# Six hosted matmul groups packed into 16 rounds each: a hybrid attention and short-convolution block on one core

## The chip, the cores and the metric

The program runs on one core of a Trainium2 chip. The metric is the device time of one execution in microseconds (us). The engines are TensorE (PE, matmuls, with its weight loads listed apart as PEld), VectorE (DVE), ScalarE (ACT), GpSimd (POOL) and SyncE (SP, which here only issues DMAs). Each works through its own list in order and waits on semaphores for the others.

## The reference

One layer of a streaming encoder. 16 meta tokens are put ahead of 256 input rows of width 2048, the rows are RMS-normalised, and one large projection makes everything that follows:

```
h = rmsnorm(x, norm_g)
proj = einsum('bld,dn->bln', h, w_in)          # w_in: 2048 x (10 * 2048 + 16)
(q, k, v, f_logit, z_att, u, gate_b, gate_c, z_conv, m_att, m_conv) = split(proj)
y_att  = (forgetting_attention(q, k, v, log_sigmoid(f_logit + b_f)) * silu(z_att)) @ w_att_o
y_conv = (gate_b * short_conv(gate_c * u, conv_w) * silu(z_conv)) @ w_conv_o
merged = sigmoid(m_att) * y_att + sigmoid(m_conv) * y_conv
return x + merged @ w_out                      # then a last rmsnorm
```

All data are float32. The kernel gets float32 accuracy out of a rounded format by splitting each operand into a high and a low part and summing three products: high x high, high x low, low x high.

## The kernel before

The part that the change touches is the first half of the program, the short-convolution stage. Its work comes in **units**. A unit is 512 KB of `w_in` (four blocks of 128 rows, 256 columns). For each unit SP loads it into one of 4 raw buffers (`load_conv`), ACT copies it to the rounded high part `w_hi` (L651), DVE subtracts to get the low part `w_lo` (L1025), and PE multiplies (24 matmuls of 258 columns on L1445 to L1447 in a pair's first 8 units, 16 on L1459 and L1460 in its last 8). 16 units make one **pair** of 128-channel blocks: u, gate_c, gate_b and z_conv with 4 units each. There are 8 pairs, 128 units. Around a pair's units lie small side operations on ACT and DVE that take the projections out of PSUM and do the convolution: on DVE `cu` (L1128), two adds (L1146, L1148), two operations on `joined` (L1132, L1135), one more (L1139), the gate (L1152, L1154) and the low part of the result (L1158).

Three other projections, m_conv, m_att and z_att, do not have a stage of their own. They are **hosted**: cut into six **groups** of 1024 columns, computed by a seven-product scheme for 2 x 2 blocks (Strassen's, in Winograd's form), and inserted between the units of the convolution. A group has 16 **steps**, one after a unit. The first 8 steps (its A half, at the rounds in `A_AFTER`) have 9 matmuls of 512 columns each, the last 8 (the B half, `B_AFTER`) have 12. Here a **round** is one unit with the step behind it, if it has one; the number of a round counts from the group's first unit. A step's weights (a quad of four 512-column blocks) are loaded into one of 3 buffers, DVE forms sums of blocks in place (one sum, L1037, in an A step; three that follow one another, L1039, L1041, L1043, in a B step), ACT rounds (L659 and L663, or L667 and L670), and DVE splits (L1050 and L1055, or L1059 and L1062).

The products of a group add up in four PSUM banks (P1, P2, P5, P7). Between its halves ACT copies P1 and P5 out (L742, L745) and DVE adds P2 (L1166, semaphore `c11_made`) before PE may begin the B half. At the group's end ACT copies P1 (L751, semaphore `u2_kept`), DVE makes four blocks (L1173, L1176, L1180, L1184; `c21_made` comes with the third), and PE may begin the next group. These places are set by `group_at(n, offset)`: ACT and DVE do them in round `offset` of the group, after that round's own rounding and splitting.

What sets the order is a set of tables and the loops over n in each engine's block: `GROUP_UNITS`, `A_AFTER`, `B_AFTER`, and `sums_after`, which says in which round of DVE the parts of a step's sum are made. In DVE's loop a round is: sums, the unit's split, the step's splits, side operations of the pair, and then the copies out of a group. ACT and DVE run ahead of PE, but at most five slots: `w_hi` and `w_lo` have `CONV_RING` = 5 slots in this stage, a unit takes one and a step two, and ACT waits on `w_used` for the slot five before.

Before the change a group takes `GROUP_UNITS` = 18 units. 16 have a step behind them; the units of round 8 and round 17 are **free**, with no step. After the six groups (units 16 to 123) four units are left.

Of the kernel before, what the change touches and what calls it, by code (L numbers as in the profile page):

```python
# [65 lines left out]
N_CONV, N_F, N_ATT, N_OUT = 4 * PER, 2, 3 * PER, 2 * KT  # L66
# [1 line left out]


GROUPS, GROUP_COLS = 6, 1024  # L70
GROUP_UNITS = (CONV_UNITS - N_CONV) // GROUPS
STEPS = KT // 2
A_AFTER = (0, 1, 2, 3, 4, 5, 6, 7)
B_AFTER = (9, 10, 11, 12, 13, 14, 15, 16)
STEP_AFTER = A_AFTER + B_AFTER
GROUP_SLOTS = GROUP_UNITS + 2 * len(STEP_AFTER)
CONV_RING, QUADS = 5, 3
# [88 lines left out]
def group_at(n, offset):  # L166

    g, r = divmod(n - N_CONV - offset, GROUP_UNITS)
    return g if r == 0 and 0 <= g < GROUPS else None
# [33 lines left out]
def hybrid_block(nc, x, meta_tokens, norm_gain, w_in, b_f, conv_w, w_att_o, w_conv_o, w_out,  # L203
# [131 lines left out]
    with ExitStack() as ctx:  # L335
# [258 lines left out]
        def _(act):  # L594
# [88 lines left out]
            for n in range(LEAD + 1, CONV_UNITS + LEAD + 1):  # L683
# [50 lines left out]
                if n == 14:  # L734
                    round_sum(S4, sum_t0[:, 1, :, :])

                g = group_at(n, A_AFTER[-1] + 2)
                if g is not None:
                    act.wait_ge(w_used, RING + step_slot(g, STEPS - 1) + 2)
                    if g > 0:  # L740
# [2 lines left out]
                    if g > 0:  # L743
                        act.wait_ge(c22_made, g)
                    nc.scalar.copy(p5[:], ps[:, P5_BANK, :]).then_inc(p5_kept, 1)  # L745
                g = group_at(n, B_AFTER[-1] + 2)
                if g is not None:
                    act.wait_ge(w_used, RING + step_slot(g, 2 * STEPS - 1) + 2)
                    if g > 0:
# [150 lines left out]
        def _(dve):  # L900
# [210 lines left out]
            for n in range(LEAD + 1, CONV_UNITS + LEAD + 1):  # L1111
# [48 lines left out]
                                            ).then_inc(o_split, 1)  # L1160
                make_sums(n)

                g = group_at(n, A_AFTER[-1] + 2)
                if g is not None:
                    dve.wait_ge(p1_kept, g + 1)
                    nc.vector.tensor_tensor(stage[0][:], stage[0][:], ps[:, P2_BANK, :], ALU.add  # L1166
                                            ).then_inc(c11_made, 1)
                g = group_at(n, B_AFTER[-1] + 2)
                if g is not None:
                    dve.wait_ge(u2_kept, g + 1)  # L1170
                    if g > 0:
# [205 lines left out]
        def _(pe):  # L1377
# [144 lines left out]
            def strassen_step(g, step):  # L1522

                c, s = step_slot(g, step), step % STEPS
                first, last_one = s == 0, s == STEPS - 1
                left, right = slice(0, HALF), slice(HALF, UNIT)
                one = lambda cols: (w_hi[:, hi_slot(c), cols], w_lo[:, lo_slot(c), cols])
                two = lambda cols: (w_hi[:, hi_slot(c + 1), cols], w_lo[:, lo_slot(c + 1), cols])
                p1, p2, p5_, p7 = (ps[:, bank, :] for bank in (P1_BANK, P2_BANK, P5_BANK, P7_BANK))
                if step < STEPS:  # L1530
                    if first:
                        pe.wait_ge(s_split, 1)
                        if g > 0:
                            pe.wait_ge(c21_made, g)
                    pe.wait_ge(w_split, RAW + c + 1)
                    product(p1, *h_piece(0, 2 * s), *one(left), start=first, stop=last_one)
                    product(p2, *h_piece(0, 2 * s + 1), *one(right), start=first, stop=last_one).then_inc(w_used, 1)
                    pe.wait_ge(w_split, RAW + c + 2)
                    product(p5_, *sum_piece(S1, s), *two(left), start=first, stop=last_one).then_inc(w_used, 1)
                else:  # L1540
                    if first:
                        pe.wait_ge(s_split, 4)
                        pe.wait_ge(c11_made, g + 1)
                        pe.wait_ge(p5_kept, g + 1)
                    pe.wait_ge(w_split, RAW + c + 1)
                    product(p1, *sum_piece(S2, s), *one(left), start=False, stop=last_one, resumed=True)
                    product(p7, *sum_piece(S3, s), *one(right), start=first, stop=last_one).then_inc(w_used, 1)
                    pe.wait_ge(w_split, RAW + c + 2)
                    product(p2, *h_piece(1, 2 * s + 1), *two(left), start=first, stop=last_one)
                    product(p5_, *sum_piece(S4, s), *two(right), start=False, stop=last_one, resumed=True  # L1550
                            ).then_inc(w_used, 1)
# [182 lines left out]
```

## Time and profile before

| | us |
|---|---|
| median of 3 runs (lowest, highest) | 1215.01 (1214.58, 1215.49) |
| the profiled execution's own time | 1215.36 |
| its span, first to last instruction | 1213.4 |
| PE busy | 1196.0 |
| DVE busy | 956.8 |
| ACT busy | 649.9 |

The span is cut by the profiler's first and last instruction; the 2 us between it and the execution's own time lie around it. A matmul that follows another is started before that one has ended, so starts, not durations, show how fast PE goes. A row of the timeline gives the start in us from the span's start, the duration, the engine and line, what is written and read, and in brackets the idle time just before it and what ended it.

### The profile page before, as it was taken

The numbers are of one execution on the slowest core, as the hardware profiler recorded it, in microseconds if no ns is written. First come the engines' busy times: TensorE is split into PE (matmuls) and PEld (weight loads), VectorE is DVE, ScalarE is ACT, GpSimd is POOL, SyncE is SP. The second block draws the span as 40 slices with busy tenths as digits, with TensorE's granted clock in tenths as the row PEclk, the third lists the DMA queues.
The fourth block names the chain that finished last, engine by engine and source line by source line (L and its number), as shares of the span: only waits on it lengthen the run. The fifth ranks groups of instructions, "written<-read, shape, count | busy, mean of one in ns | idle before, by whom it ended". The sixth has DMA issues, their size and how long they took to land.

```text
span 1213.4 us, 18388 instructions
## 1 busy us (share of the span) xinstructions
PE 1196.0 (99%) x7225; PEld 1068.2 (88%) x7225; DVE 956.8 (79%) x1116; ACT 649.9 (54%) x865; POOL 35.7 (3%) x50
## 2 busy tenths in 40 slices
PE   7999999999999999999999999999999999999997
PEld 7998898898888988889888899999999999888885
DVE  6889988988989989989966546877787778755544
ACT  6666555556656566656555444444544554543532
POOL 1000000000000000000000010111011101000000
PEclk9999999999999999999999999999999999999999
DMA  6798898897898888888677866555655565765663
GB/s 215 217 299 279 268 295 268 272 302 258 272 291 286 269 293 282 271 302 265 196 240 262 269 187 182 149 171 168 208 153 172 152 204 164 224 207 178 214 227 114
DMA packets 181393, 280.40 MB, mean 231 GB/s; under 512 B 9312, under 2 KB 128176, under 8 KB 180912
## 3 DMA queue, kind: packets, MB, share of 16 engines
q1 hardware_dynamic: 172000, 263.78, 68.2%
q10 hardware_dynamic: 9312, 15.49, 4.1%
q8 instruction: 57, 0.93, 0.3%
q14 instruction: 24, 0.20, 0.1%
HBM read 270.83 MB, written 8.41 MB: 230 GB/s over the span
## 4 chain that ended last, share of the span: by engine, by line
PE 89%; DVE 8%; issue 1%; ACT 1%; DMA 0%; POOLq 0%; POOL 0%; SPq 0%; DVEq 0%; ACTq 0%
PE ps L1445 22%; PE ps L1447 22%; PE ps L1446 22%; PE ps L1459 13%; PE ps L1460 7%; DVE w_lo L1025 2%; DVE w_lo L1062 1%; DVE w_lo L1059 1%; DVE quads L1041 1%; DVE quads L1043 1%; DVE quads L1039 1%; DMA x_nat<-in_x 0%; PE ps L1468 0%; PE ps L1439 0%; PE ps L1613 0%
## 5 line engine op out<-in xcount | busy, mean ns | idle before, releaser
L909 DVE TENSOR_TENSOR w_lo<-w_raw,w_hi 128x1024 fp32r<-128x1024 f32 x197 | 239.7, 1235 | 99.1 <-ACT w_hi L603 98.4
L1445 PE MATMUL ps<-h,w_hi 128*128 128x258 f32 (+1 forms) x1024 | 294.2, 287 | 1.6 <-DVE w_lo L1025 0.9
L1446 PE MATMUL ps<-h,w_hi 128*128 128x258 f32 (+1 forms) x1024 | 291.7, 285 | 0.0
L1447 PE MATMUL ps<-h,w_lo 128*128 128x258 f32 (+1 forms) x1024 | 291.5, 285 | 0.0
L1459 PE MATMUL ps<-h,w_hi 128*128 128x512 f32 x768 | 273.3, 398 | 0.3 <-DVE w_lo L1025 0.3
L603 ACT CAST w_hi<-w_raw 128x1024 fp32r<-128x1024 f32 x198 | 203.3, 1049 | 112.6 <-PE ps L1447 65.6
L1460 PE MATMUL ps<-h,w_lo 128*128 128x256 f32 x768 | 215.4, 280 | 0.0
L1445 PEld LDWEIGHTS ps<-h,w_hi 128*128 128x128 f32 x1024 | 193.3, 189 | 5.4 <-issue 1.9
L1446 PEld LDWEIGHTS ps<-h,w_hi 128*128 128x128 f32 x1024 | 193.5, 189 | 1.9
L1447 PEld LDWEIGHTS ps<-h,w_lo 128*128 128x128 f32 x1024 | 193.4, 189 | 0.0
L1459 PEld LDWEIGHTS ps<-h,w_hi 128*128 128x128 f32 x768 | 144.2, 188 | 35.5 <-DVE w_lo L1025 1.0
L1025 DVE TENSOR_TENSOR w_lo<-w_raw,w_hi 128x1024 fp32r<-128x1024 f32 x122 | 148.7, 1220 | 16.1 <-ACT w_hi L651 16.0
L1460 PEld LDWEIGHTS ps<-h,w_lo 128*128 128x128 f32 x768 | 145.0, 189 | 1.8
L651 ACT CAST w_hi<-w_raw 128x1024 fp32r<-128x1024 f32 x122 | 126.9, 1050 | 25.6 <-PE ps L1447 25.6
L667 ACT CAST w_hi<-quads 128x1024 fp32r<-128x1024 f32 x48 | 50.6, 1053 | 109.3 <-DVE quads L1041 102.2
L1445 PE MATMUL ps<-w_hi,o 128*128 128x512 f32 x256 | 100.2, 391 | 0.0
L1447 PE MATMUL ps<-w_hi,o 128*128 128x512 f32 x256 | 99.7, 389 | 0.0
L1446 PE MATMUL ps<-w_lo,o 128*128 128x512 f32 x256 | 99.6, 389 | 0.0
L1445 PE MATMUL ps<-w_hi,s_hi 128*128 128x512 f32 x192 | 75.6, 394 | 0.0
L1447 PE MATMUL ps<-w_hi,s_lo 128*128 128x512 f32 x192 | 75.3, 392 | 0.0
L1446 PE MATMUL ps<-w_lo,s_hi 128*128 128x512 f32 x192 | 74.8, 390 | 0.0
L663 ACT CAST w_hi<-quads 128x512 fp32r<-128x512 f32 x48 | 29.8, 622 | 64.0 <-PE ps L1447 32.2
(197 smaller groups left out, 1827.5 us busy)
## 6 DMA issues: line engine op xcount, KB each, us to landing
w_raw<-in_w_in SPq DMA_DIRECT2D x226, 512.0 KB, 4.8
quads<-in_w_in SPq DMA_DIRECT2D x144, 512.0 KB, 4.4
w_raw<-in_w_conv_o SPq DMA_DIRECT2D x32, 512.0 KB, 5.6
w_raw<-in_w_att_o SPq DMA_DIRECT2D x32, 512.0 KB, 4.8
w_raw<-in_w_out SPq DMA_DIRECT2D x32, 512.0 KB, 4.7
quads<-in_w_in SPq DMA_DIRECT2D x48, 256.0 KB, 4.7
gates_dram<-stage ACTq DMA_DIRECT2D x24, 256.0 KB, 4.8
gate_nat<-gates_dram ACTq DMA_DIRECT2D x8, 512.0 KB, 4.2
```

What stands on the lines that cost most here:

```text
L603: nc.scalar.copy(w_hi[:, hi_slot(c), :], w_raw[:, c % RAW, :]).then_inc(w_rounded, 1)
L651: nc.scalar.copy(w_hi[:, hi_slot(c), :], w_raw[:, n % RAW, :]).then_inc(w_rounded, 1)
L663: nc.scalar.copy(w_hi[:, hi_slot(c + 1), 0:HALF], quads[:, q, 0, HALF:]).then_inc(w_rounded, 1)
L667: nc.scalar.copy(w_hi[:, hi_slot(c), :], quads[:, q, 0, :]).then_inc(w_rounded, 1)
L909: nc.vector.tensor_tensor(w_lo[:, lo_slot(c), :], w_raw[:, c % RAW, :], w_hi[:, hi_slot(c), :].bitcast(F32), ALU.subtract).then_inc(w_spli ...
L1025: nc.vector.tensor_tensor(w_lo[:, lo_slot(c), :], w_raw[:, n % RAW, :], w_hi[:, hi_slot(c), :].bitcast(F32), ALU.subtract).then_inc(w_spli ...
L1039: nc.vector.tensor_tensor(b12, b22, b12, ALU.subtract).then_inc(t_made, 1)
L1445: nc.tensor.matmul(dst, a_hi, b_hi, start=start, stop=False, skip_group_check=resumed)
L1446: nc.tensor.matmul(dst, a_hi, b_lo, start=False, stop=False, skip_group_check=resumed)
L1447: return nc.tensor.matmul(dst, a_lo, b_hi, start=False, stop=stop, skip_group_check=resumed)
L1459: nc.tensor.matmul(dst, a_hi, b, start=start, stop=False)
L1460: return nc.tensor.matmul(dst[:, HI, :], a_lo, b[:, HI, :], start=False, stop=stop)
```

## The change

A group takes 16 units, each with a step, so there are no free units: the B half is in rounds 8 to 15, and the next group follows at once. The groups then lie on the pairs, units 16 to 111, and the last pair's 16 units have no group. The copies out of PSUM move from two rounds after a half's last step to one round after. The wait for `c21_made` at a group's first step moves from its first product to its second; the first product now waits for `u2_kept`. With `B_AFTER` beginning right behind `A_AFTER`, the function `sums_after` puts all three parts of the first B step's sum in round 8 itself.

```diff
@@ -68,10 +68,10 @@
 
 
 GROUPS, GROUP_COLS = 6, 1024
-GROUP_UNITS = (CONV_UNITS - N_CONV) // GROUPS
+GROUP_UNITS = 16
 STEPS = KT // 2
 A_AFTER = (0, 1, 2, 3, 4, 5, 6, 7)
-B_AFTER = (9, 10, 11, 12, 13, 14, 15, 16)
+B_AFTER = (8, 9, 10, 11, 12, 13, 14, 15)
 STEP_AFTER = A_AFTER + B_AFTER
 GROUP_SLOTS = GROUP_UNITS + 2 * len(STEP_AFTER)
 CONV_RING, QUADS = 5, 3
@@ -734,7 +734,7 @@
                 if n == 14:
                     round_sum(S4, sum_t0[:, 1, :, :])
 
-                g = group_at(n, A_AFTER[-1] + 2)
+                g = group_at(n, A_AFTER[-1] + 1)
                 if g is not None:
                     act.wait_ge(w_used, RING + step_slot(g, STEPS - 1) + 2)
                     if g > 0:
@@ -743,7 +743,7 @@
                     if g > 0:
                         act.wait_ge(c22_made, g)
                     nc.scalar.copy(p5[:], ps[:, P5_BANK, :]).then_inc(p5_kept, 1)
-                g = group_at(n, B_AFTER[-1] + 2)
+                g = group_at(n, B_AFTER[-1] + 1)
                 if g is not None:
                     act.wait_ge(w_used, RING + step_slot(g, 2 * STEPS - 1) + 2)
                     if g > 0:
@@ -1160,12 +1160,12 @@
                                             ).then_inc(o_split, 1)
                 make_sums(n)
 
-                g = group_at(n, A_AFTER[-1] + 2)
+                g = group_at(n, A_AFTER[-1] + 1)
                 if g is not None:
                     dve.wait_ge(p1_kept, g + 1)
                     nc.vector.tensor_tensor(stage[0][:], stage[0][:], ps[:, P2_BANK, :], ALU.add
                                             ).then_inc(c11_made, 1)
-                g = group_at(n, B_AFTER[-1] + 2)
+                g = group_at(n, B_AFTER[-1] + 1)
                 if g is not None:
                     dve.wait_ge(u2_kept, g + 1)
                     if g > 0:
@@ -1531,9 +1531,11 @@
                     if first:
                         pe.wait_ge(s_split, 1)
                         if g > 0:
-                            pe.wait_ge(c21_made, g)
+                            pe.wait_ge(u2_kept, g)
                     pe.wait_ge(w_split, RAW + c + 1)
                     product(p1, *h_piece(0, 2 * s), *one(left), start=first, stop=last_one)
+                    if first and g > 0:
+                        pe.wait_ge(c21_made, g)
                     product(p2, *h_piece(0, 2 * s + 1), *one(right), start=first, stop=last_one).then_inc(w_used, 1)
                     pe.wait_ge(w_split, RAW + c + 2)
                     product(p5_, *sum_piece(S1, s), *two(left), start=first, stop=last_one).then_inc(w_used, 1)
```

How this moves instructions is shown at three places. `quads` is the buffer of a step's weights, `w_hi` and `w_lo` the two parts, `ps` PSUM.

DVE in group 0 where the B half begins. Before, two units (two L1025) lie between the start of the first sum and the step's splits:

```order
L1039 TENSOR_TENSOR quads<-quads 128x512 [waits quad_landed2]
L1041 TENSOR_TENSOR quads<-quads 128x512 [waits t_made]
L1025 TENSOR_TENSOR w_lo<-w_raw,w_hi 128x1024 [waits w_rounded]
L1043 TENSOR_TENSOR quads<-quads 128x512 [waits t_made]
L1025 TENSOR_TENSOR w_lo<-w_raw,w_hi 128x1024 [waits w_rounded]
L1059 TENSOR_TENSOR w_lo<-quads,w_hi 128x1024 [waits w_rounded]
L1062 TENSOR_TENSOR w_lo<-quads,w_hi 128x1024 [waits w_rounded]
L1128 TENSOR_TENSOR cu<-ps,u_sb 128x516 [waits free_a,w_used]
L1166 TENSOR_TENSOR stage_90<-stage_90,ps 128x512 [waits p1_kept]
```

and after the change:

```order
L1039 TENSOR_TENSOR quads<-quads 128x512 [waits quad_landed2]
L1041 TENSOR_TENSOR quads<-quads 128x512 [waits t_made]
L1043 TENSOR_TENSOR quads<-quads 128x512 [waits t_made]
L1025 TENSOR_TENSOR w_lo<-w_raw,w_hi 128x1024 [waits w_rounded]
L1059 TENSOR_TENSOR w_lo<-quads,w_hi 128x1024 [waits w_rounded]
L1062 TENSOR_TENSOR w_lo<-quads,w_hi 128x1024 [waits w_rounded]
L1166 TENSOR_TENSOR stage_90<-stage_90,ps 128x512 [waits p1_kept]
L1039 TENSOR_TENSOR quads<-quads 128x512 [waits quad_landed0]
```

One L1025 is gone, the three parts of the sum stand together ahead of the unit, and the copy out (L1166) comes before the side operation L1128, which has moved into the next round.

DVE at the end of group 0. Before:

```order
L1025 TENSOR_TENSOR w_lo<-w_raw,w_hi 128x1024 [waits w_rounded]
L1139 TENSOR_TENSOR joined<-ps,joined 128x512 [waits low_kept]
L1037 TENSOR_TENSOR quads<-quads 128x512 [waits z_joined,quad_landed1]
L1025 TENSOR_TENSOR w_lo<-w_raw,w_hi 128x1024 [waits w_rounded]
L1050 TENSOR_TENSOR w_lo<-quads,w_hi 128x1024 [waits w_rounded]
L1055 TENSOR_TENSOR w_lo<-quads,w_hi 128x512 [waits w_rounded]
L1173 TENSOR_TENSOR stage_91<-stage_92,ps 128x512 [waits u2_kept]
L1176 TENSOR_TENSOR stage_92<-stage_92,ps 128x512 [waits c12_made]
L1180 TENSOR_TENSOR stage_90<-stage_92,ps 128x512 [waits gate_stored0,v_made]
L1184 TENSOR_TENSOR stage_92<-stage_92,p_93 128x512 [waits p5_kept,c21_made]
L1037 TENSOR_TENSOR quads<-quads 128x512 [waits quad_landed2]
L1025 TENSOR_TENSOR w_lo<-w_raw,w_hi 128x1024 [waits w_rounded]
```

After the change:

```order
L1062 TENSOR_TENSOR w_lo<-quads,w_hi 128x1024 [waits w_rounded]
L1037 TENSOR_TENSOR quads<-quads 128x512 [waits quad_landed1]
L1025 TENSOR_TENSOR w_lo<-w_raw,w_hi 128x1024 [waits w_rounded]
L1050 TENSOR_TENSOR w_lo<-quads,w_hi 128x1024 [waits w_rounded]
L1055 TENSOR_TENSOR w_lo<-quads,w_hi 128x512 [waits w_rounded]
L1173 TENSOR_TENSOR stage_91<-stage_92,ps 128x512 [waits u2_kept]
L1176 TENSOR_TENSOR stage_92<-stage_92,ps 128x512 [waits c12_made]
L1180 TENSOR_TENSOR stage_90<-stage_92,ps 128x512 [waits gate_stored0,v_made]
L1184 TENSOR_TENSOR stage_92<-stage_92,p_93 128x512 [waits p5_kept,c21_made]
L1037 TENSOR_TENSOR quads<-quads 128x512 [waits quad_landed2]
L1025 TENSOR_TENSOR w_lo<-w_raw,w_hi 128x1024 [waits w_rounded]
```

The free unit (the first L1025 before) and a round with a step no longer stand ahead of L1173: the four blocks now come in the first round of the next group, and L1139 one round behind them.

PE at the first step of group 1. Before:

```order
L1447 MATMUL ps<-h,w_lo 128x258
L1445 MATMUL ps<-w_hi,h 128x512 [waits w_split,c21_made,s_split]
L1446 MATMUL ps<-w_lo,h 128x512
L1447 MATMUL ps<-w_hi,h 128x512
L1445 MATMUL ps<-w_hi,h 128x512
L1446 MATMUL ps<-w_lo,h 128x512
```

After the change:

```order
L1447 MATMUL ps<-h,w_lo 128x258
L1445 MATMUL ps<-w_hi,h 128x512 [waits w_split,u2_kept,s_split]
L1446 MATMUL ps<-w_lo,h 128x512
L1447 MATMUL ps<-w_hi,h 128x512
L1445 MATMUL ps<-w_hi,h 128x512 [waits c21_made]
L1446 MATMUL ps<-w_lo,h 128x512
```

The first product waits for ACT's copy alone, and the second for DVE's third block.

## Rows read from the trace of the kernel before

**Rows 1.** The page, section 1: busy time, share of the span and instructions.

```profile
PE 1196.0 (99%) x7225; PEld 1068.2 (88%) x7225; DVE 956.8 (79%) x1116; ACT 649.9 (54%) x865; POOL 35.7 (3%) x50
```

**Rows 2.** Waits of PE, whole span: waiting line, releaser, total us, times, longest.

```profile
PE ps L1468 <- DMA x_nat<-in_x: 7.4, 1, 7.4
PE ps L1445 <- DVE w_lo L1025: 0.9, 1, 0.9
...
PE ps L1459 <- DVE w_lo L1025: 0.3, 1, 0.3
```

**Rows 3.** Windows: length, busy PE, PEld, DVE, ACT, POOL (instructions), clock, DMA share, GB/s.

```profile
107.60:152.46 44.86, 44.86 (x235) 37.97 (x234) 44.16 (x52) 27.32 (x33) 0.00 (x0) 1.00 0.84 270
...
65.35:603.79 538.44, 537.17 (x3171) 473.97 (x3169) 497.86 (x578) 322.18 (x391) 0.00 (x0) 1.00 0.85 275
```

**Rows 4.** Timeline of PE, group 0: first matmuls of units and steps.

```profile
99.88 0.28 PE L1445 MATMUL ps<-h,w_hi 128*128 128x258 f32 x1
...
102.74 0.39 PE L1445 MATMUL ps<-w_hi,h 128*128 128x512 f32 x1
...
104.81 0.39 PE L1459 MATMUL ps<-h,w_hi 128*128 128x512 f32 x1
...
107.62 0.40 PE L1459 MATMUL ps<-h,w_hi 128*128 128x512 f32 x1
...
110.45 0.40 PE L1445 MATMUL ps<-w_hi,s_hi 128*128 128x512 f32 x1
...
113.19 0.39 PE L1459 MATMUL ps<-h,w_hi 128*128 128x512 f32 x1
...
118.79 0.39 PE L1459 MATMUL ps<-h,w_hi 128*128 128x512 f32 x1
...
135.62 0.50 PE L1459 MATMUL ps<-h,w_hi 128*128 128x512 f32 x1
```

**Rows 5.** Timeline of DVE, group 0, end of A half and B half.

```profile
99.32 0.68 DVE L1039 TENSOR_TENSOR quads<-quads 128x512 f32<-128x512 f32 x1
...
107.21 0.68 DVE L1166 TENSOR_TENSOR stage<-stage,ps 128x512 f32<-128x512 f32 x1
107.81 0.68 DVE L1039 TENSOR_TENSOR quads<-quads 128x512 f32<-128x512 f32 x1
...
109.86 1.22 DVE L1025 TENSOR_TENSOR w_lo<-w_raw,w_hi 128x1024 fp32r<-128x1024 f32 x1
...
113.27 0.68 DVE L1039 TENSOR_TENSOR quads<-quads 128x512 f32<-128x512 f32 x1
...
118.73 0.68 DVE L1146 TENSOR_TENSOR conv<-conv,conv 128x512 f32<-128x512 f32 x1
...
120.06 0.68 DVE L1039 TENSOR_TENSOR quads<-quads 128x512 f32<-128x512 f32 x1
...
130.97 0.68 DVE L1132 TENSOR_TENSOR joined<-ps,joined 128x512 f32<-128x512 f32 x1
...
132.30 0.68 DVE L1039 TENSOR_TENSOR quads<-quads 128x512 f32<-128x512 f32 x1
...
134.35 1.22 DVE L1025 TENSOR_TENSOR w_lo<-w_raw,w_hi 128x1024 fp32r<-128x1024 f32 x1
```

**Rows 6.** Timeline of ACT, group 0, where the B half begins.

```profile
103.00 1.05 ACT L667 CAST w_hi<-quads 128x1024 fp32r<-128x1024 f32 x1 [1.55 <-PE ps L1447]
...
105.33 0.58 ACT L742 COPY stage<-ps 128x512 f32<-128x512 f32 x1
```

**Rows 7.** Timeline of DVE, copies out at the end of group 0.

```profile
154.13 0.68 DVE L1173 TENSOR_TENSOR stage<-stage,ps 128x512 f32<-128x512 f32 x1
...
156.89 0.69 DVE L1037 TENSOR_TENSOR quads<-quads 128x512 f32<-128x512 f32 x1
...
160.37 0.68 DVE L1152 TENSOR_TENSOR gate<-joined,gate 128x512 f32<-128x512 f32 x1
```

**Rows 8.** Timeline of PE, group 2, the longest wait of the stage.

```profile
328.60 0.36 PE L1445 MATMUL ps<-h,w_hi 128*128 128x258 f32 x1 [0.85 <-DVE w_lo L1025]
```

## The prediction

> **What bounds the kernel now.** I read the page first: PE is busy for 1196.0 of 1213.4 us and DVE for 956.8 [rows 1]. Then the waits of PE: of the little idle time 7.4 us is the first load, and only 1.2 us lies in the stage that hosts the groups, both times behind DVE's split of a unit, L1025 [rows 2]. Then the windows: over the hosted stretch, 65.35 to 603.79, PE is busy for all but 1.27 us, while in a B half (107.60 to 152.46) DVE is busy for 44.16 of 44.86 us, 98% [rows 3]. So PE sets the end everywhere, with DVE right behind it in the B halves. The change removes no matmul and adds none. It can give back at most the 1.3 us of waits, and the question is how much lead over PE it takes from DVE.
>
> **The two paces.** From the starts in PE's timeline [rows 4]: a unit of 24 matmuls takes 102.74 - 99.88 = 2.86 us, one of 16 takes 107.62 - 104.81 = 2.81, an A step 104.81 - 102.74 = 2.07 (nine matmuls, 0.23 each), a B step 113.19 - 110.45 = 2.74, and a whole B round 118.79 - 113.19 = 5.60. From DVE's starts [rows 5]: a B round takes 113.27 - 107.81 = 5.46, namely 2.05 for the three sums (to 109.86) and 3.41 for three splits, 1.14 each. A 512-column operation by itself takes 0.60 (107.21 to 107.81); the pair's side operations that come two by two take 1.33 (118.73 to 120.06, and 130.97 to 132.30). An A round takes DVE 160.37 - 156.89 = 3.48 [rows 7] against PE's 4.93. So in a B round DVE gains 0.14 us, and every side operation in a B half costs lead. DVE starts a B half with all the lead that the five slots allow: ACT itself waited 1.55 us for PE there [rows 6].
>
> A rule speaks of just this number. The Trainium skill says in "VectorE: DVE Perf Modes", section "The DRAIN you can't avoid", that the next operation does not start until the pipeline is empty. The splits here last 1.22 us and start 1.14 apart [rows 5], so the trace does not bear it out. By the rule a B round would cost DVE about 0.26 us more (three splits by 0.08), some 12 us over 48 rounds. I go by the starts.
>
> **Check of the method on before.** Unit 10 of group 0 starts at 113.19 [rows 4], and its split is done at 109.86 + 1.22, seen by PE about 0.05 later: a lead of 2.06 us. To unit 14 DVE needs four rounds and two double side operations, 4 x 5.46 + 2 x 1.33 = 24.5, PE 22.4: a loss of 2.10. The lead should be just gone at unit 14. It is: the split of unit 14 ends at 134.35 + 1.22 = 135.57 [rows 5], and PE starts it at 135.62, its first matmul 0.50 instead of 0.39 long [rows 4].
>
> **Part 1: no free unit before the B half.** Up to 99.32, where DVE begins the first B step's sum, nothing changes in group 0. Then, after the change: three sums to 101.37, the unit's split to 102.51, the step's first split to 103.65. The second waits for ACT's rounding, which waits for the slot of unit 7: done at 102.74, seen 0.26 later as in [rows 6], rounding 1.05, so DVE goes on at 104.09 and is through at 105.23. Next is the copy out L1166. It waits for ACT's copy of P1, which needs the last A step (done at 104.81): 104.81 + 0.26 + 0.58 + 0.04 = 105.69. DVE idles 0.46, and begins the sums of round 9 at 106.29. The bank is ready at 106.4, and PE begins the B half at 104.81 + 2.81 = 107.62, so this wait costs PE nothing. Unit 9 is split at 106.29 + 2.05 + 1.22 + 0.05 = 109.61, and PE wants it at 107.62 + 2.74 = 110.36. The lead is 0.75 us, where it was 2.06 at the matching place.
>
> From unit 9 to unit 14 DVE needs 5 x 5.46 + 0.60 + 1.33 + 1.33 = 30.56 us (L1128 now lies behind unit 9) and PE 28.00, a loss of 2.56. PE must wait 2.56 - 0.75 = 1.8 us per B half: by rounds 0.75 at unit 12, behind the two adds, and 1.05 at unit 14, behind the two operations on `joined`. All six groups have this alignment, since group and pair both take 16 units.
>
> **Part 2: the copies out in the next group's first round.** PE ends the B half at T, then does unit 0 (2.86) and step 0 (2.07), and wants unit 1 at T + 4.93. DVE has done unit 0's splits and stands at L1173 until ACT has copied P1: T + 0.26 + 0.58 + 0.04. Its four operations take 156.89 - 154.13 = 2.76 [rows 7]. The third, which releases the second product of step 0, ends at about T + 3.05. PE reaches step 0 at T + 2.86 and that product 0.69 later, so the moved wait hides it; with the old wait it would cost 0.2 us at each of five places. What is queued behind is the sum (0.60) and the split of unit 1, seen at T + 0.88 + 2.76 + 0.60 + 1.27 = T + 5.5. PE waits 0.6 us, in five groups. After this the A half lets DVE win back about 1.45 us a round, so the next B half begins from full slots again.
>
> **Part 3: behind the last group** no step follows unit 0 of the last pair, so PE wants unit 113 at T + 2.86, while its split (no sum ahead) is there at T + 4.9: a wait of 2.05, once. The other 15 plain units cost DVE 1.14 each plus side operations against PE's 2.8, and nothing waits. The loads move with their rounds. Each quad still waits for the splits of the step three before; SP has no new order within a round, and the DMA share of the stage is 0.85 [rows 3]. I cost them at nothing; two rounds of DVE, 10.9 us, lie between that split and the next use of the buffer, which hides them.
>
> **Sum.** 5 x (1.8 + 0.6) + 1.8 + 2.05 = 15.8 us of waits by starts. Before has 1.27 idle, and each wait also hides what is left of the matmul before it (0.39 - 0.23 = 0.16), with smaller ones not visible: I take 2.0, within 1.3 and 2.7. Net +13.8. The profiled execution took 1215.36, its span 1213.4 and 2 us around it that do not change: 1229.1. It lies 0.35 above the median of the runs, so I forecast 1228.8.
>
> What no row shows is DVE at L1166 waiting for ACT. Its idle could be from 0 (ACT's copy is ready, as it was before) to 1.05 (one more rounding ahead of it), 0.46 from the rows; that is -0.5 to +0.6 on each of six leads, -3 to +4 us. The wait at L1173 has bounds of 0 idle (the unit's split and 0.6 us of wait gone: -3 - 0.9) and the same 1.05 more (+6). Both ends together are unlikely.
>
> **Rivals.**
> Not slower: the lead at unit 9 stays as deep as the slots allow. If DVE had 2.56 us or more there, all six B halves would run as group 0 does now, groups 1 and 2 would lose their waits of today, and the time would be 1215.0 - 1.3 = 1213.7, or within 0.2% with the waits of part 2. For it speaks that group 0, with this alignment, has almost none today. Against it speaks where the lead comes from: the free unit gives PE 2.81 us of work and DVE 1.14, and that goes. It decides at 2.56 against my 0.75.
>
> Half the price: only one of the two waits of a B half appears and ACT's copies come early, 7 us: 1222.
>
> The banks become the bound: if the copies out end a microsecond later than worked out, PE waits at 11 half-group starts for the bank itself and DVE starts each half with 1 us less lead. That is 11 us more: 1240. The margins against it are 1.2 us at the B half and 0.5 at the second product.
>
> The clock: the longest wait of the stage now, 0.85 us [rows 8], left the granted clock at 1.00, 2.4 GHz, over the whole stretch [rows 3]. If some 18 waits of 0.6 to 2 us each brought one round at the lower level, twice as long, that would be 18 x 5.6 = 100 us, 1329. The Trainium skill, in "TensorE: Matmul & The Clock Gate", section "A second HAM failure mode: psum-queue depth-cycling", tells of a kernel whose frequent short idles between groups of matmuls made the clock swing. By that rule this would be the outcome; the trace does not show it so far.
>
> **How the numbers follow.** The forecast has 0.74, not slower 0.06 (half of it within 0.2%), half the price 0.09, the banks 0.09, the clock 0.02. About 0.2%, 2.4 us, is what a measurement can tell. Faster 0.03, same 0.04, slower 0.93. The forecast's own range is 1225 to 1233; half the price and part of the banks' case widen it to 1222 to 1235.
>
> **What would show it.** In the profile after: waits of PE for L1025 of some 15 us in total, three in each group (units 12, 14, and 1 of the next), and one of about 2 us in the last pair; DVE without idle in the B halves but for about 0.5 us at L1166; a clock of 1.00; no wait on L1166 or L1180. Wrong would be: no waits at units 12 and 14, PE waits released by stage copies, or a growth outside the hosted stretch.

## The result, and the profile after

The changed kernel takes 1230.56 us, median of 4 runs (1228.49 to 1230.96), against 1215.10 of the kernel before in the same rounds (1214.58 to 1215.49): 1.0124 times as long, 95% interval 1.0112 to 1.0136. It is slower by 15.5 us, where 13.8 were forecast. The profiled execution took 1230.9 us, its span 1228.9.

Line 1 of the page after, to be held against [rows 1]:

```profile
PE 1200.9 (98%) x7225; PEld 1068.9 (87%) x7225; DVE 958.5 (78%) x1116; ACT 648.8 (53%) x865; POOL 35.7 (3%) x50
```

The counts of instructions have not changed. On the chain that ended last DVE's share rose from 8% to 18%, PE's fell from 89% to 78%.

```profile
PE 78%; DVE 18%; issue 2%; ACT 1%; DMA 0%; POOLq 0%; POOL 0%; SPq 0%; DVEq 0%; ACTq 0%
```

The waits of PE in the profile after (line, releaser, total, times, longest). Against 1.2 us in the hosted stretch before [rows 2] there are 12.1, in 18 places, all behind DVE's split of a unit:

```profile
PE ps L1459 <- DVE w_lo L1025: 8.4, 12, 0.8
PE ps L1468 <- DMA x_nat<-in_x: 7.3, 1, 7.3
PE ps L1445 <- DVE w_lo L1025: 3.7, 6, 1.8
```

The stage they are in, from the windows of the profile after (stretch, its length, busy PE, PEld, DVE, ACT, POOL, granted clock, DMA share, GB/s). The first row is the six groups. The second is the first eight units of the last pair, and the third a piece of that, whose granted clock is 0.57 on average: for 3.41 of its 3.94 us the clock was at the lower of the two levels (1.2 instead of 2.4 GHz). The last row is all that follows the convolution:

```profile
65.29:584.39 519.10, 508.83 (x2930) 442.89 (x2929) 481.29 (x559) 304.80 (x369) 0.00 (x0) 1.00 0.84 275
584.39:610.89 26.50, 24.67 (x193) 24.45 (x192) 15.83 (x17) 12.50 (x15) 0.00 (x0) 0.94 0.70 218
589.26:593.20 3.94, 3.94 (x20) 3.94 (x21) 3.54 (x4) 2.53 (x3) 0.00 (x0) 0.57 0.69 178
633.50:1228.90 595.40, 587.39 (x3586) 528.05 (x3584) 398.26 (x453) 282.55 (x405) 31.62 (x34) 1.00 0.61 190
```

From the first hosted unit to the end of the convolution the kernel before takes 617.91 - 65.35 = 552.56 us, the changed one 633.50 - 65.29 = 568.21: 15.65 us more. The rest takes 595.5 in both (1213.4 - 617.9 and 1228.9 - 633.5). So the whole difference lies in the hosted stretch and the last pair.

Inside a group, PE's starts in group 0 of the profile after (start, duration, instruction; in brackets the idle time before it and what ended it):

```profile
110.34 0.39 PE L1459 MATMUL ps<-h,w_hi 128*128 128x512 f32 x1
...
121.53 0.39 PE L1459 MATMUL ps<-h,w_hi 128*128 128x512 f32 x1
...
127.91 0.47 PE L1459 MATMUL ps<-h,w_hi 128*128 128x512 f32 x1 [0.62 <-DVE w_lo L1025]
...
133.58 0.39 PE L1459 MATMUL ps<-h,w_hi 128*128 128x512 f32 x1
...
140.06 0.50 PE L1459 MATMUL ps<-h,w_hi 128*128 128x512 f32 x1 [0.72 <-DVE w_lo L1025]
...
151.30 0.28 PE L1445 MATMUL ps<-h,w_hi 128*128 128x258 f32 x1
...
156.76 0.39 PE L1445 MATMUL ps<-h,w_hi 128*128 128x258 f32 x1 [0.37 <-DVE w_lo L1025]
```

These are units 9, 11, 12, 13, 14, and 0 and 1 of the next group. A B round is 5.60 us of PE's work [rows 4]. The round from 121.53 to 127.91 takes 6.38, the one from 133.58 to 140.06 takes 6.48: PE loses 0.78 and 0.88 us. From 151.30 to 156.76 it needs 5.46 for work of 4.93: 0.53 lost. The brackets show less (0.62, 0.72, 0.37), since the matmul ahead of a wait is drawn out to its full 0.39 us, of which 0.16 lie beside the next one when nothing waits. The sum is 2.2 us. The groups' starts lie 86.01 us apart once and then 86.57 to 86.64, against 8 x 4.93 + 8 x 5.60 = 84.2 of work: 2.4 us a group.

DVE's timeline of the same place, to be held against [rows 5]:

```profile
99.27 0.68 DVE L1039 TENSOR_TENSOR quads<-quads 128x512 f32<-128x512 f32 x1
...
102.45 1.22 DVE L1059 TENSOR_TENSOR w_lo<-quads,w_hi 128x1024 fp32r<-128x1024 f32 x1
104.02 1.23 DVE L1062 TENSOR_TENSOR w_lo<-quads,w_hi 128x1024 fp32r<-128x1024 f32 x1 [0.35 <-ACT w_hi L670]
105.57 0.69 DVE L1166 TENSOR_TENSOR stage<-stage,ps 128x512 f32<-128x512 f32 x1 [0.32 <-ACT stage L742]
106.17 0.68 DVE L1039 TENSOR_TENSOR quads<-quads 128x512 f32<-128x512 f32 x1
...
108.22 1.22 DVE L1025 TENSOR_TENSOR w_lo<-w_raw,w_hi 128x1024 fp32r<-128x1024 f32 x1
```

The two idles of 0.35 and 0.32 are the waits for ACT that the working had put at 0.44 and 0.46. The split of unit 9 ends at 109.44 and PE wants it at 110.34: a lead of 0.85 us, once 0.05 is taken off for the signal. Before it was 2.06 us at the matching place.

### The profile page after: what moved, and what is told of

The parts are those of the page before. It is cut to its first block, busy times and chain, and to the rows that moved or that the text cites. A ratio compares the mean times of both kernels' runs of the same rounds, so it can differ in the third digit from the quotient of the medians.

```text
span 1228.9 us, 18388 instructions
## 1 busy us (share of the span) xinstructions
PE 1200.9 (98%) x7225; PEld 1068.9 (87%) x7225; DVE 958.5 (78%) x1116; ACT 648.8 (53%) x865; POOL 35.7 (3%) x50
## 4 chain that ended last, share of the span: by engine, by line
PE 78%; DVE 18%; issue 2%; ACT 1%; DMA 0%; POOLq 0%; POOL 0%; SPq 0%; DVEq 0%; ACTq 0%
PE ps L1445 20%; PE ps L1447 20%; PE ps L1446 20%; PE ps L1459 10%; PE ps L1460 5%; DVE w_lo L1025 4%; DVE w_lo L1062 3%; DVE w_lo L1059 2%; DVE quads L1041 2%; DVE quads L1043 2%; DVE quads L1039 2%; DMA x_nat<-in_x 0%; PE ps L1468 0%; DVE stage L1173 0%; DVE stage L1176 0%
## 5 line engine op out<-in xcount | busy, mean ns | idle before, releaser
L1445 PE MATMUL ps<-h,w_hi 128*128 128x258 f32 (+1 forms) x1024 | 295.3, 288 | 4.3 <-DVE w_lo L1025 3.7
L1445 PEld LDWEIGHTS ps<-h,w_hi 128*128 128x128 f32 x1024 | 194.0, 189 | 9.0 <-DVE w_lo L1025 6.0
L1025 DVE TENSOR_TENSOR w_lo<-w_raw,w_hi 128x1024 fp32r<-128x1024 f32 x122 | 148.4, 1220 | 14.9 <-ACT w_hi L651 14.6
L1445 PE MATMUL ps<-w_hi,o 128*128 128x512 f32 x256 | 100.2, 391 | 0.0
L1445 PE MATMUL ps<-w_hi,s_hi 128*128 128x512 f32 x192 | 75.8, 395 | 0.0
```

The lines of the kernel that those rows point to most:

```text
L1025: nc.vector.tensor_tensor(w_lo[:, lo_slot(c), :], w_raw[:, n % RAW, :], w_hi[:, hi_slot(c), :].bitcast(F32), ALU.subtract).then_inc(w_spli ...
L1445: nc.tensor.matmul(dst, a_hi, b_hi, start=start, stop=False, skip_group_check=resumed)
```

## The experiments

The kernels ran in three batches, each beside runs of the kernel before, with medians of 1214.66, 1214.84 and 1214.56 us. Ratios are to these, with 95% intervals.

**The changed kernel again.**

> The changed kernel again, unchanged, as the yardstick of this chip and to see the clock. Theory: the last pair's single wait of 1.8 us idle lets TensorE's clock fall for 3.41 us in most executions, and one without the fall is some 1.6 us faster (1228.5 to 1229 us at a mean clock of 0.998) than one with it (1230.2 to 1231 us at 0.995 to 0.996). If the spread of the earlier runs has another cause, time and mean clock will not go together.

Measured: 1228.83 us (1228.65 to 1230.25), ratio 1.0122 (1.0105 to 1.0139). Its waits are those of the first profile to 0.2 us. What differs most is the last pair. The windows of this run's profile, over the eight units and over the piece behind the 1.8 us wait:

```profile
584.02:609.00 24.98, 23.14 (x194) 22.93 (x192) 15.83 (x17) 12.49 (x15) 0.00 (x0) 1.00 0.74 230
588.89:592.80 3.91, 3.91 (x32) 3.91 (x33) 3.50 (x4) 2.52 (x3) 0.00 (x0) 1.00 0.69 185
```

Here 32 matmuls run in 3.91 us at the full clock, in the first profile 20 in 3.94 at the lower one, and the eight units take 24.98 instead of 26.50. So the fall costs 1.5 us, and it is no fixed part of the kernel. The expectation had it in most executions. Of these four, the profiled one did not have it, and three lie within 0.3 us of each other (1228.65 to 1228.91). Without the fall the changed kernel takes 1228.8 us. This run is what the others are compared with below.

The mean clock of a whole run, which the expectation wanted to go by, does not tell where the clock fell. The profile after has a second low piece ahead of the hosted stretch, and the profile before, in which nothing was changed, has one in the same place. Windows of the first and of the second:

```profile
16.35:19.76 3.41, 3.41 (x19) 3.41 (x18) 3.41 (x10) 2.30 (x6) 0.00 (x0) 0.50 0.07 11
```
```profile
16.30:19.71 3.41, 3.41 (x18) 3.41 (x18) 3.41 (x10) 2.31 (x6) 0.00 (x0) 0.50 0.06 9
```

The repetition has none there. So its span is shorter than that of the first profile (1226.7 against 1228.9) by more than the last pair's fall: 1.5 us are that fall, 0.4 lie in the last pair's other eight units (22.61 against 22.18 us, cause open), 0.7 ahead of the first hosted unit (65.29 against 64.56), and the six groups take 0.4 us more in the repetition (519.46 against 519.10).

**The last group's copies out one round later.** Only for the group that no group follows.

```diff
+def copies_at(n):
+
+    g = group_at(n, B_AFTER[-1] + 1)
+    if g == GROUPS - 1:
+        return None
+    return GROUPS - 1 if group_at(n, B_AFTER[-1] + 2) == GROUPS - 1 else g
...
-                g = group_at(n, B_AFTER[-1] + 1)
+                g = copies_at(n)
```

> The changed kernel, with the copies out of the last group alone made one round later on ACT and DVE, so that unit 113 is split before them. My theory: the wait of 2.0 us at unit 113 goes, unit 114 gets no new one (its split is seen at T + 4.85, wanted at T + 5.7), and with the wait goes the fall of the clock: 3.6 us less than the changed kernel, about 1227.0, and a mean clock of 0.998 in every run. If the clock fell for another reason (what lies behind the last group, or the sum of the small waits), 2.0 us less, about 1228.6, and still a fall. If the wait was the load's and not the split's place in the order, no difference.

Measured: 1226.95 us (1226.47 to 1227.54), ratio 1.0101 (1.0084 to 1.0118). The waits of PE in this profile (its lines are 8 further down):

```profile
PE ps L1467 <- DVE w_lo L1033: 8.4, 12, 0.8
PE ps L1453 <- DVE w_lo L1033: 1.9, 5, 0.4
```

Of six waits on the second line five are left, and the longest is 0.4 instead of 1.8. The eight units take 22.87 us, by their starts 585.03 and 607.90, instead of 24.98. So part 3 is right: L1173 to L1184 ahead of unit 113's split cost 2.0 us, once. The time is the expected 1227.0, but that is 1.9 us less than the repetition; the expected 3.6 counted from 1230.6 and had the clock's fall in it. As the repetition has no fall either, this run does not show that the wait brings it.

**The groups ten units later in the pairs.** Groups and units stay as after the change; only the side operations of a pair fall into other rounds.

```diff
+FIRST_HOST = N_CONV + 10
-    if n < N_CONV:
+    if n < FIRST_HOST:
...
-    return divmod(n - N_CONV, GROUP_UNITS) if N_CONV <= n else (-1, n)
+    return divmod(n - FIRST_HOST, GROUP_UNITS) if FIRST_HOST <= n else (-1, n)
```

> The changed kernel with all groups begun 10 units later (units 26 to 121), everything else equal: the same 16 rounds, but in a B half DVE now has the gate's two operations in round 9, L1158 in round 12 and L1128 in round 15, instead of L1128, two adds and two operations on joined in rounds 9, 11 and 13. My theory (pace and lead of DVE): lead 0.85 us at unit 9, then 1.33 + 0.60 of side operations less 0.14 a round before unit 13: 0.5 us of waits per B half instead of 1.7 to 1.8, so 7.5 us less than the changed kernel, about 1223. Rival (what matters is that steps follow without a free unit: banks, loads or the five slots): the waits stay whatever the side operations do, 1230.

Measured: 1224.11 us (1223.12 to 1225.77), ratio 1.0083 (1.0067 to 1.01). Its waits:

```profile
PE ps L1460 <- DVE w_lo L1026: 5.0, 6, 1.9
PE ps L1446 <- DVE w_lo L1026: 1.5, 6, 0.2
```

The kernel is 4.7 us faster than the repetition, where 7.5 were expected, and a group takes 85.70 us instead of 86.70. By PE's starts against a round's work (5.59 to 5.61 us in a B half, 4.91 to 4.93 in an A half), the six B halves lose 4.4 us in all where the repetition loses 11.3. That is 0.7 a group; the expectation had 0.5. But unit 1 of the next group now loses 0.75 instead of 0.54, and once 1.03: 4.0 in all instead of 2.7. So where the side operations fall decides some 60% of what the B halves lose and, with what is lost again at unit 1, about a third of the whole price. The rival, under which the waits stay whatever the side operations do, is out.

**The old wait back.** PE waits for `c21_made` at the first product again.

```diff
-                            pe.wait_ge(u2_kept, g)
+                            pe.wait_ge(c21_made, g)
...
-                    if first and g > 0:
-                        pe.wait_ge(c21_made, g)
```

> The changed kernel with the wait for c21_made back on the first product of a group's first step. My prediction counted 0.2 us at each of five places for this, about 1 us in all (1231.5). From the trace of the changed kernel I now think nothing is lost: PE would begin the step some 0.15 us later, but then waits 0.15 us less for unit 1, whose split DVE sets: 1230.5, the same group length of 86.6 us.

Measured: 1229.16 us (1228.13 to 1229.8), ratio 1.0122 (1.0105 to 1.0139), and groups 86.70 us apart, as in the repetition. The waits:

```profile
PE ps L1459 <- DVE w_lo L1025: 8.5, 12, 0.8
PE ps L1445 <- DVE w_lo L1025: 1.8, 1, 1.8
```

The five waits at unit 1 are gone and the time stays as it was: the later start of step 0 only uses up the time in which PE would have waited for unit 1. Moving the wait was worth nothing.

**The two adds left out.** The conv taps' two sums on DVE (L1146, L1148).

```diff
-                    nc.vector.tensor_tensor(conv[0][:], conv[0][:], conv[1][:], ALU.add).then_inc(conv_step, 1)
-                    dve.wait_ge(conv_step, steps + 1)
-                    nc.vector.tensor_tensor(conv[0][:], conv[0][:], conv[2][:, :, 0:SEQ], ALU.add
-                                            ).then_inc(conv_step, 1)
+                    dve.sem_inc(conv_step, 2)
```

> The changed kernel without the pair's two adds (L1146, L1148), on any engine; the sums over the three taps are left out of the output. After the adds on GpSimd made the kernel slower (1231.5), this tells the cause apart. My theory: a B-half wait is DVE's work less its lead, so 1.33 us less per group: no wait at unit 12, about 0.4 at unit 14, 8 us less than the changed kernel: 1221. If ACT's rounding or the banks set units 12 and 14, no change: 1229.

Measured: 1221.77 us (1220.28 to 1222.76), ratio 1.0055 (1.004 to 1.0071). Its waits, and PE at unit 14:

```profile
PE ps L1442 <- DVE w_lo L1025: 3.7, 6, 1.8
PE ps L1456 <- DVE w_lo L1025: 1.6, 6, 0.3
```
```profile
137.59 0.50 PE L1456 MATMUL ps<-h,w_hi 128*128 128x512 f32 x1 [0.27 <-DVE w_lo L1025]
```

The wait at unit 12 is gone and that at unit 14 down to 0.27 us, 0.42 by starts, as expected; a group takes 85.30 us, where it takes 86.63 in the first profile and 86.70 in the repetition: 1.33 to 1.40 less. Two such operations cost DVE 1.33 [rows 5], so they are passed on to PE in full. The six groups together are 8.2 us shorter than in the repetition. The median is lower by only 7.1: in the profiled run (1221.63) the clock fell behind the last pair's 1.8 us wait too, which costs 1.5.

**One operation twice, in the B half and in the A half.** A 512-column product repeated at L1135 (round 13, inside the B half) and, in another kernel, at L1154 (round 3, inside the A half).

```diff
+                    nc.vector.tensor_tensor(conv_gated[:], joined[:], conv[0][:], ALU.mult).then_inc(twice, 1)
+                    dve.wait_ge(twice, pair + 1)
```
```diff
+                    nc.vector.tensor_tensor(prod2[:], gate[:], conv_gated[:], ALU.mult).then_inc(twice, 1)
+                    dve.wait_ge(twice, pair + 1)
```

> The changed kernel with L1135 done twice (round 13, inside every B half). My theory: DVE has no lead left there, so the second time costs its full 0.72 us in each of six groups and nothing in the first and last pair: 4.3 us more, 1233.1. If the slots hid it: 1229.

> The changed kernel with L1154 done twice (round 3, inside every A half). The same length of work on the same engine, 0.72 us in five A halves. My theory: DVE gains 1.45 us of lead a round there and starts the B half from full slots all the same: no change, 1228.8. If the group's whole DVE work set its length, 3.6 us more: 1232.4.

Measured: in the B half 1233.36 us (1232.64 to 1233.97), ratio 1.015 (1.0134 to 1.0165); in the A half 1228.41 (1227.62 to 1229.65), ratio 1.0114 (1.0099 to 1.013). The waits of the first and of the second:

```profile
PE ps L1462 <- DVE w_lo L1026: 12.7, 12, 1.5
PE ps L1448 <- DVE w_lo L1026: 3.7, 6, 1.8
```
```profile
PE ps L1462 <- DVE w_lo L1026: 8.4, 12, 0.8
PE ps L1448 <- DVE w_lo L1026: 3.7, 6, 1.8
```

The same kind of work costs 4.5 us in one place and nothing in the other. A part of the 4.5 is the clock, which fell in the profiled run (1233.97; the two fastest are 1232.64 and 1232.78). By their starts (64.32 and 588.01) the six groups take 523.69 us instead of 519.46: 4.2 more, 0.70 for each. Unit 14's wait grew from 0.8 to 1.5. This is the plainest evidence for the account by leads: DVE's work counts in the B half, and not in round 3 of the A half, where DVE has time to spare. (Right behind the copies, in rounds 0 and 1, it counts too, as the waits at unit 1 show.)

**A free unit back, in the middle or at the end.** Groups of 17 units. In the first kernel the free unit stands before the B half, in the second between the groups.

```diff
-GROUP_UNITS = 16
+GROUP_UNITS = 17
-B_AFTER = (8, 9, 10, 11, 12, 13, 14, 15)
+B_AFTER = (9, 10, 11, 12, 13, 14, 15, 16)
...
-                g = group_at(n, A_AFTER[-1] + 1)
+                g = group_at(n, A_AFTER[-1] + 2)
```
```diff
-GROUP_UNITS = 16
+GROUP_UNITS = 17
...
-                g = group_at(n, B_AFTER[-1] + 1)
+                g = group_at(n, B_AFTER[-1] + 2)
```

> Half of the change: groups of 17 units with the free unit before the B half put back (B half in rounds 9 to 16, copies two rounds behind the A half, as before), and none between groups. My theory: the B-half waits fall from 1.8 us a group to what the kernel before has at such positions (3 us over all six, since the groups drift by one unit against the pairs), while the waits behind the copies at a group's end stay: 0.6 in five groups and 2.0 once. 1212.7 without waits + 3 + 3 + 2 = 1220.7. If the B-half waits came from the missing unit between the groups instead, it would stay near 1227.

> The other half: groups of 17 units with the free unit between groups put back, and the B half right behind the A half as in the changed kernel. My theory: no waits behind the copies at a group's end and none of 2 us at the last (5 us less than the changed kernel), B-half waits of 1.4 to 2.1 us a group, 10.8 in all: 1212.7 + 10.8 = 1223.5. The rival that the end copies set the pace: 1216 to 1218.

Measured: 1222.74 us (1222.15 to 1223.34), ratio 1.0068 (1.0053 to 1.0084), and 1224.1 us (1224.0 to 1224.26), ratio 1.0078 (1.0063 to 1.0094). The waits of the first and of the second:

```profile
PE ps L1445 <- DVE w_lo L1025: 5.3, 7, 1.8
PE ps L1459 <- DVE w_lo L1025: 1.5, 4, 0.8
```
```profile
PE ps L1459 <- DVE w_lo L1025: 6.3, 9, 1.1
PE ps L1445 <- DVE w_lo L1025: 0.9, 1, 0.9
```

Each free unit takes away the waits of its own kind. These rows sort by PE's line and not by place: on L1445 lie the waits at unit 1 as well as those of a B half that falls on a pair's first eight units. Such are these two, at unit 100 in the first kernel and at unit 116 in the second:

```profile
500.99 0.36 PE L1445 MATMUL ps<-h,w_hi 128*128 128x258 f32 x1 [0.87 <-DVE w_lo L1025]
```
```profile
589.74 0.36 PE L1445 MATMUL ps<-h,w_hi 128*128 128x258 f32 x1 [0.87 <-DVE w_lo L1025]
```

By PE's starts, worked out as above, the six B halves lose 11.3 us in the repetition, 4.5 with the free unit in the middle and 11.6 with the one at the end. Unit 1 of the next groups loses 2.7, 3.5 and nothing, and the 2.0 at the last group stay with the unit in the middle and go with the one at the end. So the unit at the end does nothing for the B halves, and the one in the middle nothing for unit 1. Two such units give the kernel before.

The first kernel came 2.0 us above its expectation, 1.5 of it in the B halves (4.5 instead of 3). The rest is at unit 1, where the idle time grew to 0.88 and 0.64 us in two of the drifting groups, instead of the 0.37 with the groups on the pairs:

```profile
334.47 0.36 PE L1445 MATMUL ps<-h,w_hi 128*128 128x258 f32 x1 [0.88 <-DVE w_lo L1025]
...
423.17 0.39 PE L1445 MATMUL ps<-h,w_hi 128*128 128x258 f32 x1 [0.64 <-DVE w_lo L1025]
```

**The two adds on GpSimd.**

```diff
+            for pair in range(PAIRS):
+                steps = pair * CONV_STEPS
+                pool.wait_ge(taps_made, pair + 1)
+                nc.gpsimd.tensor_tensor(conv[0][:], conv[0][:], conv[1][:], ALU.add).then_inc(conv_step, 1)
+                pool.wait_ge(conv_step, steps + 1)
+                nc.gpsimd.tensor_tensor(conv[0][:], conv[0][:], conv[2][:, :, 0:SEQ], ALU.add
+                                        ).then_inc(conv_step, 1)
```

> The changed kernel with the pair's two adds (L1146, L1148, both operands in SBUF) done by GpSimd instead of DVE; order and waits else the same. My theory (the waits of a B half are DVE's side operations less its lead): 1.33 us less of DVE work before unit 12, so the wait of 0.78 us at unit 12 goes and that at unit 14 shrinks to about 0.5; 1.3 us less in each of six groups, 8 us less than the changed kernel (1228.8), about 1221. Rival A: GpSimd and DVE get in each other's way in SBUF, the DVE operations beside an add get longer and part of the gain is lost (1224 or more). Rival B (the dense packing itself): no change.

Measured: 1231.46 us (1231.15 to 1231.95), ratio 1.0138 (1.0122 to 1.0153): slower than the changed kernel, where 8 us of gain were expected. The timeline of this profile, GpSimd first and then DVE over the same time and one round on:

```profile
117.91 1.36 POOL L578 TENSOR_TENSOR conv<-conv,conv 128x512 f32<-128x512 f32 x1 [67.87 <-ACT u_sb L724]
119.34 1.53 POOL L580 TENSOR_TENSOR conv<-conv,u_sb 128x512 f32<-128x512 f32 x1
```
```profile
117.43 0.68 DVE L1046 TENSOR_TENSOR quads<-quads 128x512 f32<-128x512 f32 x1
118.15 1.67 DVE L1048 TENSOR_TENSOR quads<-quads 128x512 f32<-128x512 f32 x1
119.86 1.57 DVE L1050 TENSOR_TENSOR quads<-quads 128x512 f32<-128x512 f32 x1
...
125.47 0.69 DVE L1048 TENSOR_TENSOR quads<-quads 128x512 f32<-128x512 f32 x1
```

DVE's sums take 1.67 and 1.57 us beside GpSimd's adds, and 0.69 alone: 1.86 us lost to save 1.33. Each ends 0.55 us after the add beside it (119.27 and 119.82, 120.87 and 121.43), and GpSimd's add had started first both times (117.91 before 118.15, 119.34 before 119.86). So DVE seems to have stood still until GpSimd was through. The Trainium skill says so in "SBUF — State Buffer", section "SBUF: two separate sides": the ports that DVE and GpSimd share are an exclusive lock, which a DVE operation with two inputs in SBUF wants as well when GpSimd's operation reads SBUF, and whichever comes second waits for the whole instruction of the first. The trace agrees. The expectation had this as its rival A, without a price: there it took part of the gain, here it took all of it and 2.6 us more.

**The kernel before with adds and gates on GpSimd.** The same edit on the kernel before, with the two products of the gate as well.

```diff
+                pool.wait_ge(conv_sig, pair + 1)
+                nc.gpsimd.tensor_tensor(gate[:], joined[:], gate[:], ALU.mult).then_inc(z_gated, 1)
+                pool.wait_ge(z_gated, pair + 1)
+                nc.gpsimd.tensor_tensor(prod2[:], gate[:], conv_gated[:], ALU.mult).then_inc(conv_step, 1)
```

> The kernel before, with the pair's two adds and the gate's two operations (L1152, L1154) on GpSimd. Its only waits in the hosted stage, 2.0 us by starts in groups 1 and 2, lie where these side operations stand in a B half; they should go: 1212.7 against 1214.7, the fastest of all. If GpSimd slows DVE by more than it takes from it, new waits of L1025 and no gain.

Measured: 1218.6 us (1217.02 to 1219.03), ratio 1.0033 (1.002 to 1.0045): slower than before by 3.8 us, as the expectation's last sentence had it. DVE's splits at L1036 take 1274 ns on average, against 1220 for L1025 before. Half of them still take 1218 ns or less, the longest 2314: it is a few of them that are held up. PE waits:

```profile
PE ps L1449 <- DVE w_lo L1036: 2.1, 2, 1.8
PE ps L1463 <- DVE w_lo L1036: 0.8, 2, 0.6
```

**The kernel before with its groups four units later.** Free units stay, only the alignment to the pairs moves, by the same constant as above.

```diff
+FIRST_HOST = N_CONV + 4
```

> The kernel before with its groups begun 4 units later (units 20 to 127), so that they meet the pairs at other places. Its waits of 2.0 us lie in groups 1 and 2, which start at units 2 and 4 of a pair; now only group 0 stands so (1.4 us). But the last group's copies come in the first round behind the stage, and PE waits for the bank before the forget-gate matmuls: about 0.3 to 1 us. Net 0 to -0.5: 1214.3 to 1214.8, no gain that can be measured.

Measured: 1214.66 us (1213.9 to 1215.38), ratio 0.9999 (0.999 to 1.0008). One wait is left where two were:

```profile
PE ps L1446 <- DVE w_lo L1026: 0.9, 1, 0.9
```

Nothing that can be measured: the idle time behind L1025 fell by 0.3 us, from 1.2 to 0.9. No version beat the kernel before.

## Why the prediction was right

By its own steps:

- **The two paces and the lead at unit 9: held.** Lead 0.75 worked out, 0.85 measured. Loss to unit 14 2.56 worked out; measured 0.85 + 0.78 + 0.88 = 2.51. The doubled operation (4.2 us by starts in the B half, none in the A half) and the adds left out (1.33 to 1.40 us a group) show that it is DVE's work there that is counted.
- **Waits at units 12 and 14: held, the split between them less well.** 0.75 and 1.05 were forecast, 0.78 and 0.88 measured. The working stopped DVE for 0.46 us at L1166, the trace for 0.32.
- **Unit 1 of the next group: held.** T + 5.5 was forecast, 5.46 measured, a wait of 0.53 instead of 0.6. Five groups start 2.4 us late, as the sum had it.
- **The moved wait: wrong.** It was to be worth 0.2 us at each of five places; with the old wait back the time is the same, within 0.3 us. A delay in front of a wait that another engine ends is swallowed by it.
- **The last pair: the wait held, the clock did not.** 2.05 forecast, 589.26 - 584.39 - 2.86 = 2.01 measured. Behind it the clock fell in the profiled run, and that costs 1.5 us which the sum lacked. The rival on the clock spoke of every wait; the 17 of up to 0.8 us left it at 1.00 [first row of the windows after], and only the longest brought it down. The low piece lasted 3.41 us and cost 1.5, where the rival had 18 rounds and 100 us. One more low piece lay ahead of the hosted stretch, before and after the change alike.
- **Before's own waits, 2.0: about right.** They can't be read by themselves, but the net can: 13.8 was forecast, and from the first hosted unit to the end of the convolution the repetition takes 631.18 - 64.56 = 566.62 us, 14.1 more than the 552.56 before. (The first profile's 15.65 has the clock's 1.5 in it.)
- **Banks, loads, instructions moved: nothing,** as costed. No wait for L1166 or L1180 appears in the trace.

So the forecast of 1228.8 is the time of the changed kernel when its clock holds (1228.83 in the repetition). The mechanism and the size of its terms are borne out; that the two agree to 0.03 us is luck, for the B halves lose 11.3 us instead of 10.8, unit 1 in five groups 2.7 instead of 3.0, and the kernel before itself had medians from 1214.56 to 1215.10. Of the 1.7 us over it in the first job, the profiled run's fall explains 1.5; the other three runs of that job have no profile. That the fall comes in some executions and not in others is shown by the profiles; what decides it is left open. Ten profiles have a wait of 1.8 us or more on PE in the hosted stage or the last pair. The clock fell behind it in three (the first profile, the one without adds, and the doubled operation in the B half). In the four profiles without such a wait it did not fall in this stretch.

The rule that the prediction weighed, from the Trainium skill's "VectorE: DVE Perf Modes", section "The DRAIN you can't avoid", would have had each B round 0.26 us dearer, and the forecast some 12 us higher, about 1241 by this estimate. The measured times lie at the forecast by starts. The same section adds that a next operation which nothing holds starts earlier, and the splits, 1.22 us long and 1.14 apart [rows 5], agree with that sentence.

## What to carry to other kernels

Where one engine paces the work and the next is at 98% beside it, work out the follower's lead at the start of the dense stretch and its loss per round: an idle slot in the pacing engine's order may be the follower's only time to catch up, and removing it moves no work and still costs. A side operation is free where the follower has time to spare before its next tight place, and costs its full start-to-start time where its lead is used up. Put a stall's price down by starts, not by the idle time shown, and before saving time ahead of a wait ask what the next wait hides anyway.

## What the runs showed of the hardware

- DVE lost more beside GpSimd than GpSimd took off it: 0.69 us became 1.67 and 1.57 for a 512-column sum of two tensors in SBUF, beside adds of 1.36 and 1.53 us.
- The granted clock fell behind a single wait of PE of 1.83 or 1.84 us in three profiles, and did not behind waits of 1.8 to 1.9 us in seven. In the first profile PE had been busy for 508.83 of the 519.10 us of the six groups before. The matmuls behind it, PE's timeline:

```profile
589.26 0.39 PE L1445 MATMUL ps<-h,w_hi 128*128 128x258 f32 x1 [1.83 <-DVE w_lo L1025]
589.48 0.29 PE L1446 MATMUL ps<-h,w_hi 128*128 128x258 f32 x1
```

  In the repetition the same wait left it at 1.00.
- The granted clock also fell for 3.41 us at 16.3 to 16.7 us, ahead of the hosted stretch, in four of fourteen profiles (before, the first one after, the last group's late copies, the groups four units later). In these four PE began the convolution's first unit at 15.8 to 16.1 us, in the other ten at 14.7 to 15.5. Why is open.
- An idle time in the records is 0.16 us shorter than what the wait costs, for 512-column matmuls that start 0.23 apart and are drawn 0.39 long.
